# First-stage order with zero spins on TensorE, and four other orders, in a hybrid stream encoder

## The reference, cut to what matters

```python
h = rmsnorm(x, norm_mix);  proj = h @ w_in            # 1024 x 3584, cut into seven parts
q_sb, k_sb, v_sb, q_hg, f_hg, i_hg, g_hg = split(proj)
o_sb = rmsnorm(stick_breaking(q_sb, k_sb, v_sb), sb_gain)   # 8 heads x 64
# stick breaking: z = q k / 8; log_keep = -softplus(z) where key < query;
#   a = exp(log_sigmoid(z) + sum of log_keep over later keys);  out = a v
log_f = logaddexp(log(lb), log1p(-lb) + log_sigmoid(f_hg));  k_hg = (1 - lb) * sigmoid(-f_hg)
# HGRN2, 4 heads, state S of 128x128: S = exp(log_f) * S + k v^T;  out = q S
o_hg = rmsnorm(hgrn2(q_hg, k_hg, i_hg, log_f, s0), hg_gain) * silu(g_hg)
x = x + concat(o_sb, o_hg) @ w_out
mk, mv = rmsnorm(mem, norm_mem_kv) @ w_mk, @ w_mv            # 256 memory tokens
x = x + softmax((rmsnorm(x) @ w_mq) mk^T / sqrt(128)) mv @ w_mo   # cross-attention, 4 heads
x = x + square(relu(rmsnorm(x) @ w_ffn1)) @ w_ffn2           # 4096 wide
y = rmsnorm(x, norm_final)
```

## Time and profile before

| | us |
|---|---|
| three runs | 1870.88 median, 1869.99 to 1876.29 |
| profiled execution, its own time | 1869.14 |
| its span in the trace | 1867.3 |
| PE busy in the span | 1799.6 (96%) |
| DVE busy | 940.5 (50%) |
| ACT busy | 687.4 (37%) |
| mean granted clock of PE | 0.984 |

### The profile page before, as it was taken

One profiled execution on the slowest core, in us unless ns is written; L12 is line 12 of the kernel. 1 busy time (PEld: TensorE's weight loads), 2 busy tenths in 40 slices (PEclk: granted clock), 3 DMA queues, 4 the chain that ended last, 5 costly groups with the idle time before them and its releaser, 6 DMA issues. The chain is left out here.

```text
span 1867.3 us, 24771 instructions
## 1 busy us (share of the span) xinstructions
PE 1799.6 (96%) x10360; PEld 1609.5 (86%) x10360; DVE 940.5 (50%) x1303; ACT 687.4 (37%) x978; POOL 23.8 (1%) x46
## 2 busy tenths in 40 slices
PE   6999999999999989999999999999999999999998
PEld 6878777889999978889887898989898989889896
DVE  5476867666766797545342643333333232333234
ACT  5577777753433455223351420202021121112122
POOL 1000000000000000000000100000000000000001
PEclk9999999999999989999998999999999999999999
DMA  5322211201121241612240111111111111111102
GB/s 189 83 80 61 57 61 46 73 26 45 37 58 36 70 144 58 263 46 68 79 125 12 52 51 46 36 32 57 34 46 45 46 44 37 34 57 34 46 23 102
DMA packets 147933, 118.52 MB, mean 63 GB/s; under 512 B 4592, under 2 KB 129008, under 8 KB 147824
## 3 DMA queue, kind: packets, MB, share of 16 engines
q1 hardware_dynamic: 147824, 116.96, 20.3%
HBM read 98.92 MB, written 18.02 MB: 63 GB/s over the span
## 5 line engine op out<-in xcount | busy, mean ns | idle before, releaser
L225 ACT ACTIVATE sbuf_w_hi<-sbuf_raw 128x1024 fp32r<-128x1024 f32 x116 | 121.8, 1054 | 382.1 <-PE PS L2023 315.7
L1977 PE MATMUL PS<-sbuf_h_hi,sbuf_w_hi 128*128 128x384 f32 x768 | 256.9, 334 | 0.0
L1979 PE MATMUL PS<-sbuf_h_hi,sbuf_w_lo 128*128 128x384 f32 x768 | 256.6, 334 | 0.0
L1978 PE MATMUL PS<-sbuf_h_lo,sbuf_w_hi 128*128 128x384 f32 x768 | 256.6, 334 | 0.0
L2022 PE MATMUL PS<-sbuf_w_hi,sbuf_u_lo 128*128 128x512 f32 x576 | 227.2, 395 | 0.0
L2023 PE MATMUL PS<-sbuf_w_lo,sbuf_u_hi 128*128 128x512 f32 x576 | 227.2, 395 | 0.0
L2021 PE MATMUL PS<-sbuf_w_hi,sbuf_u_hi 128*128 128x512 f32 x576 | 227.2, 394 | 0.0
L2075 DVE TENSOR_TENSOR sbuf_X<-PS,sbuf_X 128x512 f32<-128x512 f32 x144 | 99.4, 691 | 251.4 <-PE PS L2023 251.2
L498 PE MATMUL PS<-sbuf_h_hi,sbuf_w_hi 128*128 128x384 f32 x600 | 213.2, 355 | 6.0 <-ACT sbuf_g_N L509 3.7
L499 PE MATMUL PS<-sbuf_h_lo,sbuf_w_hi 128*128 128x384 f32 x600 | 201.8, 336 | 0.0
L500 PE MATMUL PS<-sbuf_h_hi,sbuf_w_lo 128*128 128x384 f32 x600 | 201.8, 336 | 0.0
(11 more groups left out here) (253 smaller groups left out, 2949.4 us busy)
## 6 DMA issues: line engine op xcount, KB each, us to landing
sbuf_raw<-w_ffn SPq DMA_DIRECT2D x64, 512.0 KB, 4.2
sbuf_raw<-w_in SPq DMA_DIRECT2D x28, 512.0 KB, 4.2
sbuf_X<-x_prompt SPq DMA_DIRECT2D x16, 512.0 KB, 7.9
sbuf_s_cK<-cache_sb_k SPq DMA_DIRECT2D x8, 512.0 KB, 4.8
sbuf_s_cV<-cache_sb_v SPq DMA_DIRECT2D x4, 1024.0 KB, 5.9
sbuf_raw<-w_out SPq DMA_DIRECT2D x8, 512.0 KB, 4.2
out_yp<-sbuf_X SPq DMA_DIRECT2D x8, 512.0 KB, 2.6
sbuf_r_lo<-mixT SPq DMA_DIRECT2D x7, 576.0 KB, 8.3
```

The source lines that it names most:

```text
L225: act.activation(w_hi[s][:], raw[s % 2][:], ACT.Copy).then_inc(cut_hi[s % 2], 1)
L1977: pe.matmul(out, hi, h_hi[:, kb, tok], start=kb == 0, stop=False)
L1978: pe.matmul(out, hi, h_lo[:, kb, tok], start=False, stop=False)
L1979: last = pe.matmul(out, lo, h_hi[:, kb, tok], start=False, stop=kb == KB - 1)
```

## The change

It reorders five places; the arithmetic stays.

1. First stage. SP loads the identity alone (64 KB) second, and the rest of the constants last; weight unit 2 moves ahead of X[6] in SP's list, where it waits for DVE's cut of unit 0. DVE starts without waiting for the constants. PE first runs 20 matmuls on a zeroed 128x128 tile (`spin`), 7 more behind turn 0 and 5 behind turn 2. ACT squares tiles 0 to 2 before it copies the first turned tile; weight unit 0 is cut earlier; tile 2 is turned into banks 6 and 7; the turns of tiles 4 to 8 move back by one place. Three memsets of the stick-breaking stage move to the end of this one.
2. HGRN2 head 0: ACT copies the values before the first decay exp.
3. HGRN2 last head: the last third of the values is turned into bank 7 and no longer waits for the state of head 2; level 0 starts as soon as its own third is copied. The span factors move from behind level 7 to ahead of DVE's pick of level 7.
4. Cross-attention: on PE `keys` stands ahead of `av(n - 1)`, and so do the scores of the sampled unit; on ACT `keys` stands ahead of `ex(n + 2)`.
5. Final norm: mean and scale of the last tiles are taken apart, so that tile 7's mean is made before the last addition.

The diff, cut to its core:

```diff
+        warm = s_aT[:, 0, 0:P]
         def first_pe(pe, n_mix):
-            pe.wait_ge(ld("cst"), 16)
-            for t in range(3):
-                norm_turn(pe, n_mix, t)
+            def spin(times):
+                for _ in range(times):
+                    pe.matmul(PS[:, 5, 0:P], warm, warm, start=True, stop=True)
+            pe.wait_ge(ld("warm"), 1)
+            spin(20)
+            pe.wait_ge(ld("id"), 16)
+            norm_turn(pe, n_mix, 0)
+            spin(7)
+            norm_turn(pe, n_mix, 1)
+            norm_turn(pe, n_mix, 2)
+            spin(5)
...
-                        if kb == KB // 2 and 3 + 2 * n < NT:
-                            norm_turn(pe, n_mix, 3 + 2 * n)
+                        if kb == KB // 2 and 2 + 2 * n < NT:
+                            norm_turn(pe, n_mix, 2 + 2 * n)
...
-                if n == 0:
-                    norm_turn(pe, n_mix, 3)
-                if 4 + 2 * n < NT:
-                    norm_turn(pe, n_mix, 4 + 2 * n)
+                if 3 + 2 * n < NT:
+                    norm_turn(pe, n_mix, 3 + 2 * n)
...
         def first_act(act, n_mix):
-            def between(t):
-                if t in (1, 2, 4):
-                    s = (1, 2, 4).index(t)
-                    cut_hi_unit(act, unit_sb(0, s), s)
-            norm_act(act, n_mix, between)
-            act.wait_ge(N["xn"], 4)
+            norm_square(act, n_mix, 0)
+            norm_square(act, n_mix, 1)
+            norm_square(act, n_mix, 2)
+            norm_high(act, n_mix, 0)
+            norm_high(act, n_mix, 1)
+            cut_hi_unit(act, unit_sb(0, 0), 0)
+            norm_high(act, n_mix, 2)
+            norm_square(act, n_mix, 3)
+            cut_hi_unit(act, unit_sb(0, 1), 1)
+            norm_square(act, n_mix, 4)
+            norm_high(act, n_mix, 3)
+            cut_hi_unit(act, unit_sb(0, 2), 2)
+            for t in range(4, NT):
+                if t + 1 < NT:
+                    norm_square(act, n_mix, t + 1)
+                norm_high(act, n_mix, t)
...
         def first_dve(dve, n_mix):
-            def between(t):
-                if t in (2, 3, 5):
-                    s = (2, 3, 5).index(t)
-                    cut_lo_unit(dve, unit_sb(0, s), s)
-            norm_dve(dve, n_mix, between)
+            dve.memset(warm, 0.0).then_inc(ld("warm"), 1)
+            for t in range(3):
+                norm_mean(dve, n_mix, t)
+                norm_scale(dve, n_mix, t)
+            norm_low(dve, n_mix, 0)
+            cut_lo_unit(dve, unit_sb(0, 0), 0)
+            norm_low(dve, n_mix, 1)
+            norm_mean(dve, n_mix, 3)
+            norm_low(dve, n_mix, 2)
+            norm_scale(dve, n_mix, 3)
+            norm_mean(dve, n_mix, 4)
+            cut_lo_unit(dve, unit_sb(0, 1), 1)
+            norm_scale(dve, n_mix, 4)
+            norm_low(dve, n_mix, 3)
+            norm_mean(dve, n_mix, 5)
+            cut_lo_unit(dve, unit_sb(0, 2), 2)
+            for t in range(5, NT):
+                norm_scale(dve, n_mix, t)
+                if t + 1 < NT:
+                    norm_mean(dve, n_mix, t + 1)
+                norm_low(dve, n_mix, t - 1)
+            norm_low(dve, n_mix, NT - 1)
+            dve.memset(s_QB[:], 0.0)
+            dve.memset(s_rst[:], 1.0).then_inc(ld("rst"), 1)
+            dve.wait_ge(ld("rst"), 1)
+            dve.memset(s_rst[:, 512:513], 0.0)
+            dve.wait_ge(ld("cst"), 16)
             dve.wait_ge(ld("lvl"), 16)
...
+        def norm_banks(n, t):
+            return 6 if n.first and t == 2 else 2 * (t % 2)
...
+        def values_bank(h, c):
+            return 7 if h == LASTH and c == 2 else c
...
-                    if c == 2 and h:
+                    if c == 2 and h == LASTH:
+                        pe.wait_ge(gev, hg_copied(h, 0))
+                    elif c == 2 and h:
...
-                pe.wait_ge(G["i"], h * 3 + 3)
+                if h < LASTH:
+                    pe.wait_ge(G["i"], h * 3 + 3)
                 for c, (n, t0, nt) in enumerate(lchunks):
+                    if h == LASTH and c < 2:
+                        pe.wait_ge(G["i"], h * 3 + c + 1)
+                    if h == LASTH and c == 2:
+                        pe.wait_ge(G["i"], h * 3 + 3)
+                        pe.wait_ge(G["sout"], h)
...
+            def span_decay(h):
+                act.wait_ge(G["ql"], h * NLV + NLV)
+                step(g_D[:], g_cum[:], ACT.Exp, "ecum")
+            def span_keys(h):
+                act.wait_ge(G["kdarg"], h + 1)
+                step(g_D[:], g_D[:], ACT.Exp, "kdexp")
...
                     cut_hi_unit(act, unit(R_MEM + 1, 3), 3)
+                    span_decay(LASTH)
                     mem_evict(5)
                     row_high(3)
                     row_square(3)
+                    span_keys(LASTH)
                     mem_evict(6)
...
             keys(0)
+            values(0, (0, 1, 2))
             decay(0, 1)
-            values(0, (0, 1, 2))
...
+            def span_factors(h):
+                dve.wait_ge(G["ecum"], h + 1)
...
+                ins.then_inc(G["kdarg"], 1)
+                dve.wait_ge(G["kdexp"], h + 1)
+                dve.tensor_tensor(g_kT[:], g_kT[:], g_D[:], ALU.mult).then_inc(G["kd"], 1)
...
                     cut_lo_unit(dve, unit(R_MEM + 1, 3), 3)
-                    row_low(2)
+                    span_factors(LASTH)
...
+                if h < LASTH:
+                    dve.wait_ge(G["lvl"], h * NL + NL)
+                    span_factors(h)
+                else:
+                    row_low(2)
                     cut_lo_unit(dve, unit(R_OUT, 0), 0)
-                dve.wait_ge(G["kdexp"], h + 1)
-                dve.tensor_tensor(g_kT[:], g_kT[:], g_D[:], ALU.mult).then_inc(G["kd"], 1)
...
-                sampled = n + 2 < NU and units_c[n + 2][1] == SMP
-                if n + 2 < NU and not sampled:
-                    z(n + 2)
-                if n:
-                    av(n - 1)
-                if sampled:
+                if n + 2 < NU:
                     z(n + 2)
                 if key_chunk(n) is not None:
                     keys(key_chunk(n))
+                if n:
+                    av(n - 1)
                 transposes(n)
             av(NU - 1)
...
+                if key_chunk(n) is not None:
+                    keys(key_chunk(n))
                 if n + 2 < NU:
                     ex(n + 2)
...
-                if key_chunk(n) is not None:
-                    keys(key_chunk(n))
...
-                    if g == FG - 1 and half_ and t >= 1:
+                    if g == FG - 1 and half_ and 1 <= t < NT - 2:
                         norm_step(dve, n_fin, t - 1)
                     if g == FG - 1 and (half_, t) == (1, NT - 2):
+                        norm_mean(dve, n_fin, NT - 3)
                         dve.wait_ge(fin_sq, 1)
                         dve.tensor_scalar(fin_st[:, 0:1], fin_st[:, 0:1], EPS * D, None, ALU.add).then_inc(fin_rest, 1)
                         dve.tensor_tensor(X[:, NT - 1, 0:512], X[:, NT - 1, 0:512], gain[:, 0:512], ALU.mult)\
                            .then_inc(fin_gain, 1)
+                        norm_scale(dve, n_fin, NT - 3)
+                        norm_mean(dve, n_fin, NT - 2)
...
-                    norm_step(dve, n_fin, NT - 1)
+                    dve.wait_ge(N["rs"], n_fin.base + NT - 1)
+                    last_but_one = X[:, NT - 2, :]
+                    for half_ in range(2):
...
+                        if half_ == 0:
+                            norm_mean(dve, n_fin, NT - 1)
+                    ins.then_inc(N["xn"], 1)
+                    norm_scale(dve, n_fin, NT - 1)
...
                 if t == 0:
+                    sp.dma_start(ident, a["cst"][:, C_ID:C_ID + P]).then_inc(ld("id"), 16)
                     load_gain(a["norm_mix"], D)
-                    sp.dma_start(cst[:], a["cst"]).then_inc(ld("cst"), 16)
                 if t in (2, 3):
                     feature_unit(t - 2, unit_sb(0, t - 2)[1], a["w_in"], (t - 2) * SBW)
+                if t == 5:
+                    feature_unit(2, unit_sb(0, 2)[1], a["w_in"], 2 * SBW)
+            sp.dma_start(cst[:, P:C_END], a["cst"][:, P:C_END]).then_inc(ld("cst"), 16)
             sp.dma_start(c_q[:, 0, 0:(len(LEVELS) + 1) * P], a["lvl"].rearrange("p n c -> p (n c)")).then_inc(ld("lvl"), 16)
-            feature_unit(2, unit_sb(0, 2)[1], a["w_in"], 2 * SBW)
             for s in (1, 0, 2):
                 feature_unit(s, unit_sb(1, s)[1], a["w_in"], P + s * SBW)
```

101 lines of the change are left out of this document (50 added, 51 removed).

## The result

| | us |
|---|---|
| changed kernel, four runs | 1848.03 median, 1844.25 to 1848.59 |
| kernel before, four runs beside it | 1870.77 median |
| ratio after / before, 95% interval | 0.9868, 0.9839 to 0.9896 |
| profiled execution, its own time | 1848.24 (before 1869.14) |

The forecast was 1849 in a range of 1840 to 1858.5. Between the two profiled executions the gain is 20.9 us; the sum said 22.0. The forecast added 1.7 us up to the median, because the profiled execution before lay that much under it; after, the two are alike (1848.24 and 1848.03). So the profiled execution came 1.1 us over the sum's 1847.1, and the median 1.0 under the forecast. The terms of that sum were less exact than their total, and the rows say where.

What follows compares the result with a forecast made beforehand. PE, busy 96% of the span, was taken as the bound, leaving its waits and half-clock time to win. Terms 6.4 + 2.6 + 0.8 + 5.5 + 5.5 + 1.2 = 22.0 took 1869.14 to 1847.1, plus 1.7 gave 1849, range 1840 to 1858.5.

Steps and rivals of the forecast that it cites:

- First stage: Start of the kernel: group 1 starts at 21.0 in place of 26.91; gain 6.4 us, bounds 3 and 8.5.
- I let the first scale start at 6.9: First stage: the square needs only X[0], so DVE's first scale starts at 6.9 us, before at 8.61.
- Head 0: HGRN2 head 0: ACT's value copies fit before the decay exp; gain 2.6 us, 0.9 if the remaining wait lowers the clock.
- Last head, start: HGRN2 last head: the 1.5 us state wait goes, level 0 starts at 668.8, not 669.6; gain 0.8 us.
- rival 2: Last head's end and cross-attention: the clock falls elsewhere; price 8.6 us, time 1857.5, chance 0.17.
- a sign of being wrong: Anywhere in the kernel: new stretches with the clock at 0.5 to 0.8, or a mean clock below 0.984.
- Last head, end: HGRN2 last head: earlier span factors win 2.9 us of the turned-keys wait and 2.6 of clock, together 5.5.
- Cross-attention: PE's waits for the weight copy shrink: 6.3 us gained, less 0.8 for the clock; 5.5, between 0 and 12.
- Final norm: End of the kernel: the last scale starts at 1862.2 and not 1863.43; gain 1.2 us.
- The slower rival: Cross-attention: the ring through ACT closes and units with keys pay the excess; 1876.5 us or more, chance 0.03.
- The rival on the last head's order: HGRN2 last head: the order gives nothing, the 3.0 wait reappears before the state products; price 5.5 us, chance 0.08.
- the one on the spins: First stage: the spins don't hold the clock up; price 3.3 us, time 1852, chance 0.15.

Runs made afterwards that it cites:

- e1: The changed kernel without its 32 matmuls on zeros: 1844.79 us median, ratio 0.9851 to the kernel before.
- e9: The changed kernel without spins, with head 0's weight high part before the first decay exp and the last head's memory low parts before level 4's factors: 1842.69 us.
- e6: The kernel before with only the new order of the cross-attention on PE and ACT: 1863.12 us, ratio 0.9939.
- e2: The changed kernel with the load of the gain row issued ahead of X[0]: 1844.87 us, ratio 0.9851.
- e5: The changed kernel with the last head's span factors back behind DVE's pick of level 7, on ACT and DVE: 1849.23 us, ratio 0.9868.
- e10: The changed kernel with six matmuls of 128 columns added in each of the cross-attention's four blocks of narrow matmuls: 1850.62 us, ratio 0.9885.
- e11: The changed kernel with the last head's start as before (bank 2, level 0 waiting for all three copies): 1845.97 us, ratio 0.9855.
- e7: The kernel before with only the 32 matmuls on zeros and the memset of their tile: 1867.88 us, ratio 0.9963.

## Why the prediction was right, step by step

- **First stage**, 6.4 forecast, 5.4 measured at its end. The step "I let the first scale start at 6.9" failed in this profile: not the square but the gain row holds it, at 8.67. It is met in other executions of the same order (6.93 to 7.43 in four of eight kernels). The rest of the chain held: third scale to group 1, DVE's six instructions, 8.9 forecast and 8.6 measured (13.97 to 22.52). Behind group 1 the stage gained 1.0 where the sum had 0.5. The share of the spins depends on when the clock would have risen without them: e1 gained 6.4 without spins, with an early rise, and e9 3.8, with a late one. The rule of the Trainium skill, "TensorE: Matmul & The Clock Gate", Part 4, that transposes don't count as busy for the clock, did not decide anything: the products were at full speed in every kernel with spins and the new order, and in e1 and e6 the clock rose in the third and in the second turn, with nothing but turns ahead of it (1.59 and 1.73 for the turn, and not 1.97). What the same page's Part 1 says of the start, that it varies from run to run with the same kernel, is what e1 and e9 show (group 1 at 21.44 and 24.00).
- **Stick-breaking**, no term. It took 351.8 before and 349.6 to 353.4 in the eleven others, PE's list being the same; the 1.6 given back lies in that spread.
- **Head 0**, 2.6, or 0.9 if the clock falls in the wait that is left. Both were measured: 0.9 in the profile (24.6 to 23.7 from the stage's start to level 1), 2.5 in e1, e2, e5, e10 and e11 (22.0 to 22.1). Which of the two a run gets is luck. (The 439.5 that the prediction reads for the projection before is the modelled end of level 0; the projection's own row starts at 439.13.)
- **Last head, start**, 0.8 forecast. From head 2's level 0 to level 3: 87.1 before, 85.4 after, 86.8 with the old start (e11): 1.7 in the profile, 0.4 to 1.3 by e11. The start of level 0 itself moved by the 0.7 that e11 isolates, as the forecast had it (668.8 for 669.6); the other 1.0 is clock, with level 0 at 3.19 and not 4.18. The prediction called DVE busy without a pause in the levels behind; its row says 3.12 of 4.
- **From level 3 to level 7 of the last head**, no term, and 3.0 lost (38.4 to 41.4). Half of rival 2, "the clock falls elsewhere", happened here: three falls where before two stood, and of those two one lay in level 3, where it costs nothing. These are the new stretches of low clock that the prediction named as a sign of being wrong. They need not come with the change: e1 and e10 have all of its edits here and took 38.4; four others took 40.0 to 43.0.
- **Last head, end**, 5.5 forecast, 4.5 by e5. The wait went as forecast (3.0). Of the 3.3 us of clock I had counted on winning 2.6, but 1.7 were lost again behind the keys, in the product with the values (3.07), against 3.4 before: so 1.7 were won.
- **Cross-attention**, 5.5 forecast, 11.6 measured, 10.0 by e6: the term that was mis-sized most. Its waits went from 7.7 to 1.8, so 5.9 for 6.3. Two things were missing. A wait costs more than its row says, as the kernel before shows twice behind the same four scores:

```profile
...
963.01 1.03 PE L1771 MATMUL PS<-sbuf_c_kT,sbuf_c_q 128*128 128x256 f32 x4
...
964.62 1.13 PE L1811 MATMUL PS<-sbuf_gain,sbuf_c_v 128*128 128x128 f32 x8 [0.58 <-ACT sbuf_gain L1881]
...
966.46 1.03 PE L1771 MATMUL PS<-sbuf_c_kT,sbuf_c_q 128*128 128x256 f32 x4
...
967.32 0.92 PE L1811 MATMUL PS<-sbuf_gain,sbuf_c_v 128*128 128x128 f32 x6
...
```

  (The last row is cut short by its window; only its start is used.) With a wait of 0.58 the product starts 1.61 behind the scores, without one 0.86, so the wait costs 0.75: its row begins to count only at the modelled end of the scores. Eight waits less, at 0.17 each, are 1.4 more. And I put clock at -0.8 because I couldn't tell where the falls would be; it was 147.8 x 0.06 - 136.1 x 0.04 = 3.4. About 0.9 is left without a name. Of the 11.6 the 8.2 are the order's and can be counted on; the 3.4 are where the falls lay in these two profiles, and that is luck. The rule of the Trainium skill that the prediction weighed here (same page, "Why this matters for your kernels": gaps of about 3 us bring the clock down) doesn't reach these falls: with no wait over 0.8 in this stage the clock still fell, here and in the eight other kernels with this order, so gaps are not the only cause.
- **Final norm**, 1.2 forecast, 0.9 measured, in nine kernels alike (811.1 to 810.2 or 810.3).

So 22.0 met 20.9 in part by luck: excesses of 6.1 in the cross-attention, 0.9 at the last head's start and 0.4 in the projections covered shortfalls of 1.0 at the start, 1.6 in a stage not touched, 1.7 in head 0, 3.0 and 1.0 in the last head and 0.3 at the end (to 0.1, by rounding). But for the first scale the mechanisms of the terms were right; their sizes were right only together. The slower rival (ACT's ring in the cross-attention closes) had no part: PE waited nowhere for ACT's keys or exps. The rival on the last head's order is refuted by e5, the one on the spins by the seven profiles with spins and the new order, though with the old order (e7) the clock did fall between them. The final norm and the order of loads, squares and scales in the first stage have no run of their own; their shares are read from the stretches.

## What to carry over

Price a wait of PE by the distance of the starts around it, with and without it, and not by the row alone; and where low clock stands near waits, carry both cases as a range, as the head 0 term did. Before you shorten a chain, ask which load each of its inputs really waits for: here the gain row, not the constants. When an edit is worth less than the spread of the runs (here up to 14 us), read its own stretch in several profiles, and take off what half clock cost in each: 70.7 and 71.4, 8.5 and 7.4, or 131.0 and 139.2 are told apart where medians of 1845 and 1846 are not.

## What the runs showed of the hardware

- Matmuls on a zeroed tile raise PE's clock: in all eight kernels with them the forty records of the first twenty took 6.1 to 7.6 us from 1.38 on, and the turn behind them 1.06 or 1.07 and not 1.94.
- Without them the rise came in the third turn in one kernel (e1) and only behind three turns and some sixteen products in another (e9), with the three turns starting at the same times to 0.05 us. Turns alone can raise the clock, and need not.
- With the same load list the scale that waits for the gain row started between 6.93 and 8.72 us in eight kernels, and X[0], issued 0.44 later behind the gain row (e2), was squared 2.3 to 2.6 later than in the eleven others.
- At a place that DVE sets, half clock on PE costs nothing: level 3 took 3.90 or 2.27, and the next product started 5.1 behind its start either way, in all ten kernels with the old order of that place.
